# A two-block network kernel on one core: two first products wait for their input tile by tile, a residual scaling is spread over the state tiles, and two weight loads change places in the queue

## The reference, cut to what matters

```python
# first block, expert layer: h is the normed and modulated residual
q = (h @ w_q).reshape(B, S, PEER_HEADS, 2, PEER_HALF)
...
# end of the first block: every column of the residual is scaled
return _rmsnorm(x, g_final)
...
# second block, state-space layer: u and z are halves of one product
u, z = jnp.split(h @ w_in, 2, axis=-1)
...
x_re, x_im = scan(a_re, a_im, bu_re, bu_im)      # over 256 tokens
y = einsum(x_re, c_re) - einsum(x_im, c_im) + d_skip * u
```

## Time and profile before

| What | Value |
|---|---|
| median of three runs | 3587.92 us |
| profiled execution, its own time | 3590.77 us |
| its span, first to last instruction | 3589.1 us |
| TensorE busy | 3398.9 us (95%) |
| VectorE busy | 2489.4 us (69%) |
| ScalarE busy | 1373.3 us (38%) |
| GpSimd busy | 388.2 us (11%) |
| mean granted TensorE clock | 0.981 |
| DMA, mean | 228 GB/s |

### The profile page before, as it was taken

The page is one execution under the profiler, slowest core; times in us unless marked ns, Lnnn a source line. Parts: engine busy times, 40 slices in busy tenths (PEclk is TensorE's granted clock), DMA queues, the critical chain, the costliest instruction groups (busy, mean ns, idle before and its releaser), DMA issues. The chain is left out here.

```text
span 3589.1 us, 56839 instructions
## 1 busy us (share of the span) xinstructions
PE 3398.9 (95%) x20884; PEld 3069.1 (86%) x20884; DVE 2489.4 (69%) x4546; ACT 1373.3 (38%) x1996; POOL 388.2 (11%) x401
## 2 busy tenths in 40 slices
PE   3899998999999999999999999899989899999998
PEld 2688887889877999999999998788789898999998
DVE  7666556868387777777777776888867634666665
ACT  1333311013244444444444444322244434555553
POOL 0010120000000000000000000688810000000000
PEclk8999999999999999999999999999999999999999
DMA  9678744446777888888888886122247643555543
GB/s 402 274 298 305 274 165 141 147 157 233 283 279 292 293 293 293 294 296 295 296 296 295 294 294 246 59 94 102 105 179 270 240 141 130 190 185 188 188 167 139
DMA packets 123318, 817.74 MB, mean 228 GB/s; under 512 B 12848, under 2 KB 18224, under 8 KB 27184
## 3 DMA queue, kind: packets, MB, share of 16 engines
q1 hardware_dynamic: 105696, 761.31, 58.0%
q10 hardware_dynamic: 17488, 54.58, 4.0%
HBM read 791.65 MB, written 24.18 MB: 227 GB/s over the span
## 5 line engine op out<-in xcount | busy, mean ns | idle before, releaser
L532 PE MATMUL bank<-H,ring 128*128 128x256 f32 x3680 | 821.1, 382 | 30.8 <-PEq L377 13.4
L532 PEld LDWEIGHTS bank<-H,ring 128*128 128x128 f32 x3680 | 701.5, 192 | 127.5 <-issue 25.6
L1845 DVE TENSOR_TENSOR vlo<-ring,vhi 128x1024 fp32r<-128x1024 f32 x448 | 547.5, 1225 | 289.4 <-ACT vhi L1247 287.8
L1247 ACT ACTIVATE vhi<-ring 128x1024 fp32r<-128x1024 f32 x448 | 474.0, 1060 | 607.0 <-PE bank L602 317.0
L1531 DVE TENSOR_TENSOR wlo<-ring,whi 128x1024 fp32r<-128x1024 f32 x272 | 331.9, 1231 | 324.9 <-ACT whi L1060 321.6
L568 PE MATMUL bank<-Hhi,whi 128*128 128x256 f32 x1920 | 485.7, 290 | 22.6 <-DVE Hlo L1542 10.1
L569 PE MATMUL bank<-Hlo,whi 128*128 128x256 f32 x1920 | 476.1, 285 | 0.0
L1060 ACT ACTIVATE whi<-ring 128x1024 fp32r<-128x1024 f32 x272 | 287.3, 1059 | 360.8 <-PE bank L573 322.6
L595 PE MATMUL bank<-vhi,Ghi 128*128 128x512 f32 x1024 | 402.7, 393 | 13.5 <-ACT vhi L1247 13.5
L596 PE MATMUL bank<-vhi,Glo 128*128 128x512 f32 x1024 | 401.6, 392 | 0.0
L568 PEld LDWEIGHTS bank<-Hhi,whi 128*128 128x128 f32 x1920 | 370.6, 193 | 33.0 <-issue 18.0
(11 more groups left out here) (430 smaller groups left out, 4553.4 us busy)
## 6 DMA issues: line engine op xcount, KB each, us to landing
ring<-in_peer_u SPq DMA_DIRECT2D x128, 1024.0 KB, 5.2
ring<-in_peer_v SPq DMA_DIRECT2D x128, 1024.0 KB, 5.0
arena<-in_w_mod SPq DMA_DIRECT2D x96, 1024.0 KB, 6.9
ring<-in_w_ada SPq DMA_DIRECT2D x72, 1024.0 KB, 7.4
ring<-in_w_qz SPq DMA_DIRECT2D x64, 1024.0 KB, 4.8
ring<-in_w_in SPq DMA_DIRECT2D x35, 1024.0 KB, 7.1
ring<-in_ssm_in SPq DMA_DIRECT2D x32, 1024.0 KB, 5.0
ring<-in_w_mod SPq DMA_DIRECT2D x32, 1024.0 KB, 5.7
```

What stands on the lines that cost most here:

```text
L532: last = mm(out, ring[:, pos % R, k, :], rhs[:, k, :], start=(k == 0), stop=(k == KT - 1))
L1247: A(vhi[:, half], v_half(pos, half), ACT.Copy).then_inc(s("vhi_ready"), 1)
L1845: v.tensor_tensor(vlo[:, half], v_half(pos, half), vhi[:, half].bitcast(F32), ALU.subtract)\
```

## The change

- SyncE: the skips, loads and `head_beside` of head 0 are reordered. Head 1's position 0 is now issued right behind head 0's position 5; the three `head_beside` follow; then head 0's position 7, head 1's position 1, and the last skip. The wait for `f_in_psum` is gone. VectorE runs `whole_vec` of position 5 before `vectors(0)` in head 0.
- Queries: the wait for all 16 tiles is gone; in the product at `h == 0` of both loop rounds TensorE waits before the products of tile `k` for that tile.
- State space: TensorE signals its arrival at the meet, runs the first `u` product with a wait for each tile, and only then waits for the others. ScalarE runs `u_out(0, 0)` ahead of the two tables. GpSimd waits for `y_done` and the discretised values, and clears and builds the first masks before the meet. VectorE scales the residual's tile after step 3 of each state tile.

```diff
-            for pos in range(8):
-                if pos in FIRST:
-                    head_skip(pos)
-                else:
-                    head_load(0, pos)
-            sp.wait_ge(s("f_in_psum"), 1)
+            for pos in (0, 1):
+                head_skip(pos)
+            head_load(0, 2)
+            for pos in (3, 4):
+                head_skip(pos)
+            head_load(0, 5)
+            head_load(1, 0)
             for n in range(3):
                 head_beside(0, n)
-            with sp.Fori(1, HEADS) as i:
-                for pos in range(2):
-                    head_load(i, pos)
+            head_load(0, 7)
+            head_load(1, 1)
+            head_skip(6)
+            def rest_of_head(i):
                 sp.wait_ge(s("gates_in_psum"), i + 1)
...
+            rest_of_head(1)
+            with sp.Fori(2, HEADS) as i:
+                for pos in range(2):
+                    head_load(i, pos)
+                rest_of_head(i)
...
                 for half in halves:
                     for k in range(8 * half, 8 * half + 8):
+                        if rows is not None:
+                            pe.wait_ge(s("biased"), rows + k + 1)
                         last = mm(out, ring[:, pos % R, k, :], rhs[:, k, :], ...)
...
-            pe.wait_ge(s("biased"), 2 * KT)
             pe.wait_ge(s("k_loaded"), 16)
-                    gemm("topk", i, 3 * h, banks[0][:, 0:T], 0, uses[0] + n)
+                    gemm("topk", i, 3 * h, ..., rows=KT if h == 0 else None)
...
             final_sums()
-            pe.wait_ge(s("biased"), 3 * KT)
-            meet(pe, met)
+            pe.drain().then_inc(stage_end, 1)
+            met[0] += 4
...
-            u_half(0, 0, 0)
-            u_half(0, 0, 1)
+            u_half(0, 0, 0, 2 * KT)
+            u_half(0, 0, 1, 2 * KT)
+            pe.wait_ge(stage_end, met[0])
...
+            u_out(0, 0)                       # ScalarE
             for duo in range(2):
                 table(duo, 0, duo, None)
-            u_out(0, 0)
...
+                whole_vec("heads", i, 5, 33 + 3 * i)
                 if first:
                     vectors(i)
-                whole_vec("heads", i, 5, 33 + 3 * i)
...
                     if j % 2 == 0 and not last:
                         fraction(tile + 1, duo)
+                    if j == 3:
+                        xk = x[:, bass.ds(tile, 1), :]
+                        v.scalar_tensor_tensor(xk, xk, V("g_final")[:, bass.ds(tile, 1)], rstd1, ALU.mult, ALU.mult)
...
-            for k in range(KT):
-                v.scalar_tensor_tensor(x[:, k, :], x[:, k, :], V("g_final")[:, k:k + 1], rstd1, ALU.mult, ALU.mult)
...
-            meet(pool, met)                   # GpSimd
...
+            pool.wait_ge(s("y_done"), 1)
             gp.memset(Cst_all, 0.0)
+            pool.wait_ge(s("disc_loaded"), 32)
             pool.drain()
             masks(0, 0)
+            meet(pool, met)
```

More of the change, by code:

```diff
@@ L522, in _, with gemm @@
             uses = [0, 0, 0, 0]
-            def gemm(stage, i, pos, out, bank, need=None, rhs=H, halves=(0, 1)):
+            def gemm(stage, i, pos, out, bank, need=None, rhs=H, halves=(0, 1), rows=None):
                 if need is not None:
@@ L772, in _ @@
                     n = 4 * i + h
-                    gemm("topk", i, 3 * h, banks[0][:, 0:T], 0, uses[0] + n)
+                    gemm("topk", i, 3 * h, banks[0][:, 0:T], 0, uses[0] + n, rows=KT if h == 0 else None)
                     gemm("topk", i, 3 * h + 1, banks[1][:, 0:T], 1, uses[1] + n)
@@ L848, in _, with u_half @@
             final_sums()
-            pe.wait_ge(s("biased"), 3 * KT)
-            meet(pe, met)
+            pe.drain().then_inc(stage_end, 1)
+            met[0] += 4
             pe.sem_inc(s("bu_read"), 2)
-            def u_half(i, t, half):
+            def u_half(i, t, half, rows=None):
                 b = 2 * t % 4
-                gemm("ssm", i, 2 * t, banks[b][:, 0:T], b, uses[b] + i + t // 2 if half == 0 else None, halves=(half,))
+                gemm("ssm", i, 2 * t, banks[b][:, 0:T], b, uses[b] + i + t // 2 if half == 0 else None, halves=(half,), rows=rows)
             def z_half(i, t, half):
```

## The result

The changed kernel takes 3599.95 us (median of eight runs, 3594.84 to 3605.32) against 3588.52 us (3586.68 to 3591.35) of the kernel before: a ratio of 1.0031 with a 95% interval of 1.002 to 1.0042, that is 7 to 15 us slower. Forecast were 3601 us and 12.9 us more.

What follows compares the result with a forecast made beforehand. TensorE is busy 95% of the span, but VectorE's instruction stream bounds the state tiles. Terms −4.2 − 5.9 − 4.8 + 27.8 = +12.9 us, added to 3587.9, give 3601 us; range 3588 to 3613 us.

Steps and rivals of the forecast that it cites:

- The tiles: State tiles: scaling blocked behind GpSimd 17.2 us, first fraction blocked 13.9 us, second fraction freed −3.3 us; 27.8 us slower.
- the starts: Earlier TensorE starts at head 1, the queries and the state space: gains of 4.2, 5.9 and 4.8 us.
- Queries: Queries' first product: TensorE starts on the first written tile, not after the last; gain 5.9 us, bounds 4.5 to 8.
- Weights' order: Head 1: earlier weight loads end TensorE's wait, third product near 155.8; gain 4.2 us, bounds 1.7 to 6.5.
- a bound of 1.7 us: Head 1: the gain left if the clock fell in 2.3 us of waiting and cost 2.5 us.
- State space's start: Before the state tiles: earlier first u product and table, first state multiplication at 2265.3, not 2270.11; gain 4.8 us.
- The masks: State space's start: masks lie in GpSimd's idle time before the norm; without that cover they would cost nearly 3 us.
- rival 1: State tiles: the scaling slips through unblocked and costs 4.7 us; sum −10.2, 3578 us; chance 0.20.
- Rival 2: State tiles: only the scaling is blocked, the first fraction still goes first; +2.3 us, 3590 us; chance 0.11.
- Rival 3: State tiles: the second fraction is blocked as well, another 15 us; 3616 us; chance 0.08.
- TensorE idles about 3 us a tile: State tiles: a sign expected with a period of 23.7 us instead of 21.8.
- The four terms: Weights' order −4.2, queries −5.9, state space's start −4.8, state tiles +27.8 us; sum +12.9 us.

Runs made afterwards that it cites:

- E2: Kernel before with one edit: the 16 scalings moved from the front of the state tiles to one behind step 3 of each tile; 3613.86 us (1.0065).
- E3: Changed kernel, with the tiles' scaling taking its second input from PSUM (P1 instead of rstd1) and a drain behind it; 3594.86 us (1.0014).
- E9: E8 plus, behind step 3 of each state tile, one small VectorE instruction with input and output in PSUM and a drain; 3590.48 us (1.0002).
- E10: Changed kernel with GpSimd's clearing and first masks back behind the meet; 3603.80 us (1.0043).
- E6: Kernel before with the tile-by-tile wait of the queries alone; 3584.15 us (0.9983).
- E5: Kernel before with the heads' weights' order alone (SyncE's order for head 0, VectorE's position 5 vector first); 3586.34 us (0.9989).
- E8: Changed kernel with seven scalings before the first state multiplication, none in the tiles, nine in the output product's loop; 3574.11 us (0.9955).
- E7: Kernel before with the state space's start alone, the 16 scalings left in front of the tiles; 3588.73 us (0.9994).
- E11: E8 with ScalarE's two tables ahead of its copy of the first u product again; 3578.97 us, one run.
- E1: Changed kernel with the 16 scalings back in one piece between the second fraction and the first state tile; 3578.49 us (0.9968).

## Why the prediction came out right

**The tiles: right in mechanism, in both halves, and 3.4 us too dear.** Forecast were a scaling blocked until 1.67 us behind the scans, a first fraction blocked by 0.99 us, a second freed, 23.7 us a tile. Measured: 1.69 us, 0.98 us, 0.69 us, 23.68 us. E2 shows the whole of it without the starts, E3 that two SBUF inputs are needed for the scaling's part, E3 and E9 that VectorE's lateness alone makes the fraction's part. The size was off at the edge: I counted the scaling of tile 0 and the first fraction of tile 1 as blocked, and they ran free; so did the first fraction of tile 0, which had been blocked before. E10, in which all three are blocked, takes 3.4 us more in the tiles. What I didn't see is that GpSimd, with its masks moved ahead and 31 us idle, starts 0.07 us later there.

**Queries: right, with two errors that partly cancel** (5.9 forecast, 6.2 in the changed kernel, 5.3 in E6). TensorE started 0.94 us behind ScalarE's first tile and not 0.55, and the product was out 8.6 us behind its start and not 9.3.

**Weights' order: the step that fell to a bound.** The third product starts 0.5 us later than forecast (156.30 against 155.8, in an execution in which head 0 ran 0.6 us later), and at a lower clock in part. The text had this as a bound of 1.7 us and took 4.2. The runs show either: 2.3 us in the changed kernel, 4.4 us in E5. What the 4.2 us left out is the clock: 1.4 us on the third product in six of nine profiled executions.

**State space's start: 4.05 for 4.8.** The u product started 0.65 us behind ScalarE's first tile and took 9.74 us, the dearer of the two half-clock starts and not their middle; ScalarE's copy came 10.5 us behind that first tile instead of 9.8, and the table, 0.7 us later, was late last, as forecast. The same product took 8.58 us in E8 and 10.20 us in E10, so this term can differ by over 1 us from one execution to the next. E7 confirms that the part is worth 0.7 us at most while the scalings stand in front, and E11 that ScalarE's order is needed for it.

**The masks: near in size, by luck.** I gave their cover nearly 3 us, as a delay of the first multiplication. E10 shows no such delay; what the cover is worth, 3.4 us, lies in the phase of the first tiles, which I had not thought of.

**The rivals.** The scaling never slipped through behind a scan in the loop, so rival 1 did not occur, and E3 shows that its 3578 us was too low for a scaling that does not collide. Rival 2 needs a free first fraction; it was blocked in 13 tiles, and E9 shows that 0.2 us of lateness is enough for that. Rival 3 did not occur: the second fraction stayed ahead in the last 13 tiles that have one, by 0.11 us in the tile shown above (2410.64 against 2410.75), where I had counted 0.05. That TensorE idles about 3 us a tile was too much. In this window of 13.7 tiles it idles 26.6 us, 1.9 us a tile (in the kernel before, in the same window, 8.5 us):

```profile
2275.00:2600.00 325.00, 298.43 (x1319) 249.80 (x1319) 276.71 (x441) 62.16 (x110) 269.66 (x278) 0.98 0.24 90
```

The closeness to 3599.95 us is in part two errors that cancel. The four terms measure −2.3 − 6.2 − 4.05 + 24.4 = +11.85 us against +12.9: the starts gave 2.3 us less than forecast and the tiles cost 3.4 us less. The medians lie 11.4 us apart and the profiled pair 7.7. The 4.1 us that the pair won elsewhere would make up the difference, but that they belong to these two executions alone is only argued.

## What to carry to other kernels

- When two engines share SBUF's reads, an instruction's price is not its duration but who starts first: list for each candidate place what the neighbour engine starts within 0.3 us, and put small work with two SBUF inputs where the neighbour is idle. The same 16 scalings cost 24 us in the tiles, 3.6 us in front of them (E1's first multiplication 11.06 us behind the first fraction, E8's 7.49) and at most 1 us of the start when seven lie in an idle gap (E8, where they end last by 0.97 us) and nine in a later stage.
- Look for the margin of what runs free. The first fraction was 0.1 to 0.2 us ahead of GpSimd (E8); an instruction of 0.23 us more on VectorE cost 1.0 us in each of 14 tiles.
- Measure a bundle by its parts. Here two parts gained 4 and 6 us, a third gained nothing without the fourth, and the fourth lost more than the others won; taking only its place away made the bundle 16 us faster than the kernel before.

## What the runs showed of the hardware

- A blocked VectorE instruction does not wait for the whole of GpSimd's. The scaling starts 0.17 us into a product of 1.27 us and loses 0.91 us, not 1.10; the first fraction starts 0.14 us into it and loses 0.98 us, not 1.13. The block is over 0.15 to 0.19 us before GpSimd's instruction ends by the profile. For the fraction it ends 1.12 us behind GpSimd's start whether VectorE comes 0.01 us (1.80 us in all) or 0.14 us later (1.67 us). The Trainium skill (SBUF — State Buffer, Who interferes with whom) has the first to issue keep the shared pair for its whole instruction; the measurement is a little shorter. With one input in PSUM the same instruction loses nothing (0.480 us, E3).
- GpSimd's first product starts 0.13 us behind the scans after 6 to 9 us of idling (before, E10) and 0.20 to 0.21 us behind them after 31 to 35 us (after, E1, E7, E8). The first fraction of tile 0 is blocked in all five kernels with the masks behind the meet (before, E2, E5, E6, E10: 1.80 to 1.81 us) and free in all others. That the idle time sets the 0.07 us was not tried by itself.
- The same wait of 2.7 to 2.9 us in TensorE's stream left its clock at full speed in three profiled executions (E3, E5, E10) and took it down in six, at a cost of 1.4 us. A gain of a few us that runs across such a wait has two values.
